# Expert stage 2 of a two-block model: four items of 96 and four of 64 slots in turn, and down weights joined over two buffer slots

## What is computed

```python
def moe_swiglu(h, w_router, w_gate, w_up, w_down):      # 256 tokens, D = 1024
    logits = xt @ w_router                              # 8 experts
    top_logits, top_idx = lax.top_k(logits, 2)          # two experts for each token
    gates = softmax(top_logits)
    ...                                                 # the 512 assignments, sorted by expert
    hid = silu(ragged_dot(xs, w_gate, sizes)) * ragged_dot(xs, w_up, sizes)   # 1024 -> 3584
    ys = ragged_dot(hid, w_down, sizes)                                       # 3584 -> 1024
    ...                                                 # weighted by gates, added up per token
```

## Time and profile before

| | us |
|---|---|
| median of 3 runs | 2123.65 |
| lowest and highest run | 2119.45, 2125.45 |
| span of the profiled execution, first to last instruction | 2115.7 |
| stage 2, first gather to end of the last matmul of its last down quarter | 1251.4 to 2097.0 |
| rest after it (spread of the last item, final norm, output) | 18.7 |

### The profile page before, as it was taken

How to read it: one execution, slowest core, us unless ns; L and a number is a source line. 1 busy time by engine, 2 the same in 40 slices (tenths; PEclk the granted TensorE clock), 3 DMA queues, 4 the chain that set the end, 5 groups by cost and what they waited for, 6 DMA issues and landing times.

```text
span 2115.7 us, 38813 instructions
## 1 busy us (share of the span) xinstructions
PE 1981.6 (94%) x17143; PEld 1259.4 (60%) x17143; DVE 601.3 (28%) x1071; ACT 450.6 (21%) x632; POOL 86.2 (4%) x37
## 2 busy tenths in 40 slices
PE   9989987778878999999999999999999999999998
PEld 9888543433334998999999864433343433343343
DVE  4862311111112763544475630000000010000011
ACT  4621111110112443433365320000000000000011
POOL 5420000000001000000100000000000000000000
PEclk9999988987897999999999999999999999999999
DMA  8241899999999441455633249999999999999996
GB/s 324 96 191 47 344 423 423 424 425 425 423 424 384 152 144 37 160 180 187 231 139 141 120 176 350 382 419 419 417 419 406 385 419 419 418 419 410 402 397 247
DMA packets 134767, 653.11 MB, mean 309 GB/s; under 512 B 9824, under 2 KB 32480, under 8 KB 89440
## 3 DMA queue, kind: packets, MB, share of 16 engines
q1 hardware_dynamic: 134624, 650.95, 77.2%
HBM read 649.87 MB, written 1.05 MB: 308 GB/s over the span
## 4 chain that ended last, share of the span: by engine, by line
PE 75%; DMA 16%; DVE 5%; ACT 2%; issue 1%; SPq 0%; DVEq 0%; ACTq 0%
PE psum L1971 18%; DMA ring<-in_w_gate 15%; PE psum L2034 8%; PE psum L1977 6%; PE psum L556 5%; PE psum L557 5%; PE psum L558 5%; PE psum L1676 4%; PE psum L729 3%; PE psum L2039 3%; PE psum L2306 1%; PE psum L1998 1%; PE psum L1954 1%; PE psum L590 1%; DVE arena L1179 1%
## 5 line engine op out<-in xcount | busy, mean ns | idle before, releaser
L1971 PE MATMUL psum<-ring,arena 128*32 128x384 f32 (+1 forms) x3584 | 366.4, 539 | 0.6 <-issue 0.6
L558 PE MATMUL psum<-ring_r 128*128 128x256 f32 x944 | 266.9, 283 | 0.0
L1971 PEld LDWEIGHTS psum<-ring,arena 128*32 128x32 f32 x3584 | 116.7, 110 | 214.6 <-issue 213.0
L1676 PE MATMUL psum<-ring,arena 128*32 128x512 f32 x896 | 153.9, 758 | 52.1 <-DMA ring<-in_w_gate 49.4
L2034 PE MATMUL psum<-ring,arena 128*32 128x512 f32 x1600 | 196.5, 593 | 2.3 <-ACT arena L2128 2.3
L558 PEld LDWEIGHTS psum<-ring_r 128*128 128x128 f32 x944 | 180.5, 191 | 0.0
L556 PE MATMUL psum<-ring_r 128*128 128x256 f32 x608 | 176.6, 290 | 0.3 <-DVE ring_r L620 0.3
L557 PE MATMUL psum<-ring_r 128*128 128x256 f32 x608 | 172.7, 284 | 0.0
L2195 DVE TENSOR_TENSOR arena<-arena,psum 128x512 f32<-128x512 f32 (+1 forms) x42 | 23.7, 616 | 512.4 <-PE psum L1977 326.7
L1676 PEld LDWEIGHTS psum<-ring,arena 128*32 128x32 f32 x896 | 38.9, 135 | 160.4 <-issue 158.5
L1977 PE MATMUL psum<-ring,arena 128*32 128x512 f32 (+1 forms) x1120 | 131.4, 539 | 0.0
(11 more groups left out here) (410 smaller groups left out, 2834.4 us busy)
## 6 DMA issues: line engine op xcount, KB each, us to landing
ring<-in_w_gate SPq DMA_DIRECT2D x64, 1024.0 KB, 21.5
ring<-in_moe_w_gate SPq DMA_DIRECT2D x64, 1024.0 KB, 16.4
ring<-in_moe_w_down SPq DMA_DIRECT2D x64, 1024.0 KB, 13.1
ring<-in_w_up SPq DMA_DIRECT2D x48, 1024.0 KB, 24.8
ring<-in_w_down SPq DMA_DIRECT2D x24, 2048.0 KB, 25.8
ring<-in_moe_w_up SPq DMA_DIRECT2D x48, 1024.0 KB, 16.3
ring<-in_moe_w_gate SPq DMA_DIRECT2D x64, 768.0 KB, 13.2
ring<-in_moe_w_up SPq DMA_DIRECT2D x48, 768.0 KB, 13.9
```

The costliest lines, as they stand in the source:

```text
L558: return nc.tensor.matmul(out, al, bh, start=False, stop=stop, **kw)
L1676: mm = nc.tensor.matmul(bank(0)[s * C:(s + 1) * C, :], q_Xg[:, k * PC + x * C:k * PC + (x + 1) * C], w[s][:, k, :], start=(k == 0), stop=( ...
L1971: mm = nc.tensor.matmul(bank(b0 + j)[n * MORE:(n + 1) * MORE, 0:Q], z_Xg[:, x:x + MORE], w[:, (2 * h + j) * Q:(2 * h + j + 1) * Q], start= ...
```

## The change

`ITEMS` gets four items of 96 slots (ranks 0 to 3) and four of 64 (ranks 4 to 7) in turn. The two halves of a down quarter become one load over two neighbouring slots: 2048 KB in runs of 16 KB for b0, 1536 KB in runs of 12 KB for b1. In `LOADS2` the second of the two places holds `JOINED`, for which nothing is issued, so that the numbers of slots and uses stay as they were. SyncE waits before a joined load until the later of the two slots is free. The slots' semaphores count only the loads that they get themselves. TensorE's instructions for an item of a given size, their order and their marks of use are not changed; it waits for one semaphore for each down quarter instead of two.

```diff
+JOINED = None
+DOWNS = [[x for q in quarters for x in (("d", b, q), JOINED)] for b, quarters in ((0, (0, 1)), (0, (2, 3)), (1, range(4)))]
 LOADS2 = ([("g", 0, k) for k in range(8)] + [("u", 0, k) for k in range(8)] + [("g", 1, k) for k in range(8)]
-          + [("d", 0, n) for n in range(4)] + [("u", 1, k) for k in range(8)]
-          + [("d", 0, n) for n in range(4, 8)] + [("d", 1, n) for n in range(8)])
+          + DOWNS[0] + [("u", 1, k) for k in range(8)] + DOWNS[1] + DOWNS[2])
...
-ITEMS = ((0, 96), (5, 64), (1, 96), (2, 96), (6, 64), (3, 96), (4, 96), (7, 64))
+ITEMS = ((0, 96), (4, 64), (1, 96), (5, 64), (2, 96), (6, 64), (3, 96), (7, 64))
...
+        def two_chunks(at):
+
+            n = at % SLOTS2
+            assert n % 2 == 0
+            return ring[:, SLOT_ORDER[n // 2], :] if n < 2 * SLOTS else carve(hi_at, 2 * CHUNK)
+
         def moe2_landed(i, at):
 
-            return landed2[at % SLOTS2], i * (16 * len(LOADS2) // SLOTS2) + 16 * (1 + at // SLOTS2)
+            mine = [n for n, load in enumerate(LOADS2) if load is not JOINED and n % SLOTS2 == at % SLOTS2]
+            return landed2[at % SLOTS2], i * (16 * len(mine)) + 16 * (1 + mine.index(at))
...
                 if what == "d":
-                    quarter, half = n // 2, n % 2
-                    size = Q // P * D // 2
-                    r0 = c0 + quarter * Q
-                    src = wd2[e, r0:r0 + Q, :].rearrange("e (p c) n -> p (e c n)", p=P)[:, half * size:(half + 1) * size]
+                    size = Q // P * D
+                    r0 = c0 + n * Q
+                    src = wd2[e, r0:r0 + Q, :].rearrange("e (p c) n -> p (e c n)", p=P)
+                    to = two_chunks(at)
...
-
-                    sp.wait_ge(moe2_used, i * len(LOADS2) + (at + 1 - SLOTS2))
+                    if LOADS2[at] is JOINED:
+                        continue
+                    behind = at + 1 if LOADS2[at][0] == "d" else at
+                    sp.wait_ge(moe2_used, i * len(LOADS2) + (behind + 1 - SLOTS2))
                     moe2_load(e, at)
...
-                    at = LOADS2.index(("d", b, 2 * q))
-                    for n in range(2):
-                        pe.wait_ge(*moe2_landed(i, at + n))
+                    at = LOADS2.index(("d", b, q))
+                    pe.wait_ge(*moe2_landed(i, at))
+                    w = two_chunks(at)
...
                             flat = c * D + half * 512 + n0
-                            size = n_c * D // 2
-                            return chunk(at + flat // size)[:, flat % size:flat % size + n]
+                            return w[:, flat:flat + n]
```

More of the change, by code:

```diff
@@ L454, in moe2_load @@
                     src = (wg2 if what == "g" else wu2)[e, n * P:(n + 1) * P, c0:c0 + size].rearrange("e p n -> p (e n)")
-                sp.dma_start(chunk(at)[:, 0:size], src).then_inc(landed2[at % SLOTS2], 16)
+                    to = chunk(at)
+                sp.dma_start(to[:, 0:size], src).then_inc(landed2[at % SLOTS2], 16)
             for n, slot in enumerate(SLOT_ORDER):
```

## The result

The changed kernel takes 2944.03 us (median of 4 runs, 2942.71 to 2945.65) against 2124.55 for the one before (median of 4, 2119.45 to 2126.02): 1.387 times as long, 95% interval 1.385 to 1.389. The forecast was 2113.8, faster. What came true is the last and smallest of its rivals, the second pass of eight items, priced there at 840 us.

A forecast was written before the change was run, and what follows sets the result against it. Stage 2 looked bound by TensorE, with the DMA limit almost equal (846 against 850 us). The terms -7.5 - 4.2 + 1.9 = -9.8 us took 2123.65 to 2113.8 us, range 2106 to 2121.

The forecast's parts named there:

- the second pass of eight items: Rival: in stage 2 a fifth expert with over 64 assignments adds eight items, 840 us more, 2960; chance 0.01.
- One item from 96 to 64 slots: Expert stage 2: one smaller item lets transfers set the pace and removes two dry stretches of the queue, -7.5 us.
- The set-off: Stage 2: of 36.8 us taken off TensorE, the other 29 turn into waiting for loads; waits 25 us in sum.
- The join: Stage 2 down weights: longer runs save 0.6 us per item over seven items, -4.2 us (0 to -8.4).
- I take 0: Delay of joined loads waiting for both slots in item 0: taken as hidden, 0; if not, +2.6 us once.
- The cover that I named: Start of stage 2: item 1's up weights wait for item 0's last down quarter anyway, hiding the 2.6 us delay.
- The clock: Waits for loads lower TensorE's clock; costs only at stage 2's last down quarters, 0 to 5.8 us, taken as +1.9.
- Sum for one pass: Whole kernel: -7.5 - 4.2 + 1.9 = -9.8 us, giving 2113.8 us, 0.46% less; chance 0.70.

The follow-up runs named there:

- single-pass run with the join: Changed kernel with stage 2's number of items fixed to 8, five assignments left out: 2110.99 us, ratio 0.9955 to the kernel before.

## Why the prediction was wrong

**The step that failed** is in "One item from 96 to 64 slots": "The routing allows it: the reference sends 81, 73, 71, 69, 62, 54, 52 and 50 assignments to the eight experts, so the fifth has 62, and no additional pass starts." The counts were right; "the fifth" was wrong. I took the first number of an `ITEMS` pair for the rank by count. Rank 0 belongs to expert 0 by line 97, so the rank 4 is the fourth of the others, 69. The same line also makes the sentence on the rival false, "At 62 there is room for two". Its price was right: 840 us worked out, 833.0 measured with the join (2944.03 - 2110.99) and 840.4 without (2952.21 - 2111.79). Its chance of 0.01 was the error, as was to leave untested the only assumption on which a cost of 40% hung.

**The items' sizes.** Shown right for one pass: -7.5 forecast, -7.8 in the stage's stretch (827.7 against 835.5). The set-off was only half right. From its first gather to the end of its last down quarter, stage 2 of the single-pass run with the join takes 835.0 us instead of 845.6. TensorE waits 16.9 us for loads in it (12.0, 4.0 and 0.9 in the three groups), not 25, and is busy 811.1 us instead of 838.3, so 27.2 less and not 36.8. Of the missing 9.6 us, 6.8 are three down quarters at a lower clock, see below; the rest is not assigned.

**The join.** -4.2 forecast. Per item it gives 0.7 (0.6 forecast; for all items after the start 5.5 in sum), but "I take 0" for the delay failed: the bound named there, +2.6 once, is what happened (+2.8, shown by the run with item 0 in halves). The cover that I named, the halt before item 1's up weights, comes too late: the queue was empty in item 0 itself. Net -2.7 in the trace; the medians differ by 0.8 and do not part it from nothing. The Trainium skill, "DMA: Bandwidth & Descriptors", Specifications, by which runs of 6 KB are already at line rate, is nearly right here: 106.4 to 105.7 us is 0.7%. Longer runs and fewer loads changed together, and no run parts the two. (The sum by the page is -5.6; the -5.7 there is a slip.)

**The clock.** The mechanism was right and the price at the end too high: +1.9 forecast, about 0.1 measured. Stretches of the single-pass run with the join (first row: columns as in the earlier trace rows; below it TensorE in order of time):

```profile
1640.00:1650.00 10.00, 7.29 (x44) 1.92 (x48) 0.81 (x3) 0.00 (x0) 0.00 (x0) 0.66 1.00 421
...
1642.71 9.99 PE L2045 MATMUL psum<-ring,arena 128*32 128x512 f32 x64 [3.49 <-DMA ring<-in_moe_w_down]
...
2044.41 7.05 PE L2045 MATMUL psum<-ring,arena 128*32 128x512 f32 x64
...
2086.37 2.78 PE L2045 MATMUL psum<-arena 128*32 128x512 f32 x24 [0.90 <-DMA arena<-in_moe_w_down]
```

After a wait of 3.49 us the same 64 matmuls take 9.99 us instead of 7.05, with a granted clock of 0.66; in items 5 and 7 they take 9.23 and 8.77 after waits of 5.04 and 3.50. As forecast, this costs nothing in the middle: TensorE is still ahead afterwards, and waits 0.90 us for the last load. At the end the last quarter keeps its 2.78 us, and the 72 matmuls before it (from 2077.4) take 8.05 instead of 7.93. The page's digit 9 (90% or more of full clock) hides these dips. Not every such wait lowers the clock: in the changed kernel's first pass it is 1.00 from 1640 to 1660, with a wait of 3.50 us at 1641.9. What decides was not tested.

**Sum for one pass.** -9.8 us, 0.46%, forecast; measured 0.45% (0.27 to 0.62), and -10.5 to the last landing in the trace. That it agrees so closely is in part luck: the join's gain was 1.3 larger and the clock's price 1.8 smaller than forecast, and the delay of 2.8, put at nothing, nearly makes up for both.

## What to carry to other kernels

Where a data-dependent count decides how often a stage runs, follow the count through the code's own sort key and limits to the very item, and price the miss: the gain here was 8 us, the stake 833. A change in the sizes of work items should be tried first on the list whose first item is already fixed by a prefetch; giving that item the small size, and not the fifth, brought 1.1%. And when two limits stand a few per cent apart, look at the pace of landings while the queue is full: relieving TensorE by 37 us gave 8, because the loads needed 106 us for each item where TensorE now needs 101.

## What the runs showed of the hardware

The pace of the same loads differs between the two passes. In the changed kernel's first pass every step from item 2 to item 8 is 105.6 to 105.8 us, behind large and small items alike; in the second pass it is 104.2, with the same sizes, runs and queue, and the DMA share is at its limit in both. The queues of the first pass (1454 to 1982), then of the second (2088 to 2817):

```profile
q1 hardware_dynamic: 28977, 221.51, 100.7%
q8 instruction: 42, 0.69, 0.5%
...
q1 hardware_dynamic: 40280, 308.01, 101.2%
```

In the first pass 42 packets of instructions pass through the same engines, in the second none up to 2817. Their time, 0.5% of the 16 engines' span, is 0.5 us of an item's 105.7, a third of the difference of 1.5. Item 7 is issued by the loop already, but has 6 instruction packets and the slow step of 105.6. So the instructions fit as one cause, and an even load on all engines would leave 1 us unexplained. No run here tested it, and it stays open.
